# Dense value columns of a retrieval layer: 768 columns in one fp32 product, or 1024 columns in three fp32r products of high and low parts

## The reference

```python
def chunk(zc):                                   # 128 tokens at a time
    ...                                          # expert: (128, 8, 16) indices; gate: softmax of their scores
    u = jnp.take(peer_u, expert, axis=0)
    act = jax.nn.gelu(jnp.einsum('chkd,cd->chk', u, zc))
    v = jnp.take(peer_v, expert, axis=0)
    w = (gate * act.astype(jnp.float32)).astype(zc.dtype)
    return jnp.einsum('chk,chkd->cd', w, v).astype(zc.dtype)
```

## Time and profile before

| | |
|---|---|
| median of 3 runs | 2698.61 us (2697.93 to 2700.31) |
| the profiled execution | 2700.06 us, its span 2698.2 us |
| products, 1535 to 2267 us | DVE busy 667 of 732 us, DMA share 1.01, 419 GB/s |
| dense, 2350 to 2600 us | PE busy 48.7 to 49.6 of each 50 us, DMA share 1.03, 409 GB/s |

### The profile page before, as it was taken

The page is one execution under the profiler, slowest core; times in us unless marked ns, Lnnn a source line. Parts: engine busy times, 40 slices in busy tenths (PEclk is TensorE's granted clock), DMA queues, the critical chain, the costliest instruction groups (busy, mean ns, idle before and its releaser), DMA issues.

```text
span 2698.2 us, 30775 instructions
## 1 busy us (share of the span) xinstructions
PE 2310.5 (86%) x11234; PEld 1779.3 (66%) x11234; DVE 1996.8 (74%) x2973; ACT 850.6 (32%) x1259; POOL 560.1 (21%) x706
## 2 busy tenths in 40 slices
PE   8999989999999999989899965555555656999996
PEld 7997778888888888889788832222233334655553
DVE  6986657665566556587767998889999997766667
ACT  5433555443444344454541111000233332300000
POOL 1000000000000000000002344433443442334375
PEclk9999999999999999999999976666787787999998
DMA  6533445555555655544568999999999997699998
GB/s 224 187 123 104 126 140 183 189 179 191 190 188 179 191 189 172 178 133 151 177 220 361 421 420 419 420 420 420 419 420 416 410 419 295 228 409 409 409 409 343
DMA packets 314373, 747.67 MB, mean 277 GB/s; under 512 B 21028, under 2 KB 223012, under 8 KB 275752
## 3 DMA queue, kind: packets, MB, share of 16 engines
q0 software_dynamic: 73728, 436.24, 39.6%
q1 hardware_dynamic: 240408, 309.21, 34.2%
q10 hardware_dynamic: 144, 1.05, 0.1%
HBM read 744.35 MB, written 2.10 MB: 277 GB/s over the span
## 4 chain that ended last, share of the span: by engine, by line
DMA 24%; DVE 17%; PE 13%; POOL 3%; issue 2%; ACT 1%; DVEq 0%; POOLq 0%
DMA row<-in_peer_u,expert 13%; DMA row<-in_peer_v_rows,expert 11%; DVE row L2430 8%; PE pl L832 4%; PE pl L839 3%; POOL row L770 3%; DVE acc L2441 1%; PE pl L1226 1%; PE pl L835 1%; PE pl L836 1%; DVE hot_b L2467 1%; PE pl L1155 1%; DVE wlo L1883 1%; PE pg L1251 0%; PE pl L1251 0%
## 5 line engine op out<-in xcount | busy, mean ns | idle before, releaser
L1883 DVE TENSOR_TENSOR wlo<-raw,whi 128x1024 fp32r<-128x1024 f32 (+1 forms) x436 | 517.8, 1208 | 374.1 <-ACT whi L1304 372.4
L1226 PE MATMUL pl<-row,diag 128*128 128x512 f32 (+1 forms) x666 | 403.4, 764 | 296.3 <-DMA row<-in_peer_v_rows,expert 283.5
L2430 DVE CUSTOM_DVE_ANT_0 row<-row,pg 128x2048 f32<-128x2048 f32 x256 | 576.7, 2283 | 63.3 <-DMA row<-in_peer_u,expert 62.1
L1304 ACT ACTIVATE whi<-raw 128x1024 fp32r<-128x1024 f32 (+1 forms) x436 | 444.5, 1039 | 411.2 <-PE pl L839 406.6
L1226 PEld LDWEIGHTS pl<-row,diag 128*128 128x128 f32 x666 | 167.4, 268 | 491.3 <-issue 430.3
L832 PE MATMUL pl<-x_split,whi 128*128 128x512 f32 x1888 | 478.6, 395 | 9.5 <-DVE x_split L1891 4.6
L832 PEld LDWEIGHTS pl<-x_split,whi 128*128 128x128 f32 x1888 | 341.6, 190 | 73.8 <-issue 7.5
L839 PE MATMUL pl<-x_split,wlo 128*128 128x256 f32 x2656 | 373.2, 284 | 3.8 <-DVE wlo L1883 3.8
L839 PEld LDWEIGHTS pl<-x_split,wlo 128*128 128x128 f32 x2656 | 358.6, 192 | 23.1 <-DVE wlo L1883 4.4
L770 POOL DMA_INDIRECT row<-in_peer_v_rows,expert x256 | 288.7, 1128 | 340.5 <-DVE acc L2441 147.5
L1259 PE MATMUL pg<-v_tile,spread 128*128 128x512 f32 (+1 forms) x1024 | 335.0, 489 | 4.6 <-DMA v_tile<-in_peer_v_dense 4.6
(11 more groups left out here) (337 smaller groups left out, 2136.5 us busy)
## 6 DMA issues: line engine op xcount, KB each, us to landing
raw<-in_w_in SPq DMA_DIRECT2D x51, 1024.0 KB, 5.2
v_tile<-in_peer_v_dense SPq DMA_DIRECT2D x128, 384.0 KB, 7.3
raw<-in_w_gate SPq DMA_DIRECT2D x44, 1024.0 KB, 5.1
raw<-in_w_up SPq DMA_DIRECT2D x44, 1024.0 KB, 5.1
raw<-in_w_out SPq DMA_DIRECT2D x32, 1024.0 KB, 5.5
raw<-in_w_down SPq DMA_DIRECT2D x32, 1024.0 KB, 5.4
wq<-in_peer_wq SPq DMA_DIRECT2D x15, 1024.0 KB, 11.6
raw<-in_w_down SPq DMA_DIRECT2D x16, 768.0 KB, 4.7
```

Source lines behind the costliest of these rows:

```text
L1226: last = mm(pl_all[:, c:c + width], diag[:, (at - 1) % 4, :], row[b][:, c - DENSE:c - DENSE + width], start=at == 1, stop=at == ADDED_ROWS ...
L1304: return nc.scalar.activation(o, i, ACT.Copy)
L1883: V.tensor_tensor(wlo[:, n % 4, 0:k, :], w[:, :, f, :], whi[:, n % 4, 0:k, :].bitcast(F32), ALU.subtract)\
L2430: V.tensor_tensor_reduce(row[b][:], row[b][:], z_tok[:], 1.0, 0.0, ALU.mult, ALU.add, dots[:, at:at + 1])\
```

## The change

The dense part has 1024 columns instead of 768, and is computed as three fp32r products of high and low parts instead of one fp32 product. In each of the 128 steps ACT rounds the tile (`high_tile`) and two weight blocks (`high_weights`), DVE subtracts to get the tile's low part (`low_tile`, written over the tile), POOL subtracts to get the weights' low part (`low_weights`), and PE runs high x high, high x low, low x high: 12 products of 512 columns. There are 5 tile buffers and 3 for each of the other parts. The gathered rows are 4 KB in place of 5 KB, the late ring has 5 row buffers in place of 6, PE adds 113 rows and DVE sums 143. DVE's sums now stand between its `low_tile` steps, and POOL's gathers between its `low_weights` steps, by `rows_by`. The weights `spread` lie in one tensor `spread_all`, and in the spread stage PE has three PSUM banks in turn.

```diff
-DENSE = 768
+DENSE = 1024
 GATHERED = D - DENSE
 EARLY = 100
-ADDED_ROWS = 111
+ADDED_ROWS = 113
...
+def rows_by(m):
+
+    return min(SUMMED_ROWS, (m + 1) * SUMMED_ROWS // (NKEY - 6))
...
-TILE_HOMES = RING
+TILE_HOMES = RING + 1
+HIGHS = 3
...
             sp.wait_ge(sel_ready, TT * PH)
+            sp.wait_ge(dot_done, PRODUCTS)
+            sp.wait_ge(row_added, EARLY)
             for m in range(NKEY):
                 if m == 1:
 
                     sp.wait_ge(hot_used, TT * GROUPS)
+                    sp.wait_ge(row_added, ADDED_ROWS)
                 elif m >= TILE_HOMES:
                     sp.wait_ge(tile_used, m - TILE_HOMES + 1)
...
+            def low_weights(m):
+
+                pool.wait_ge(spread_high, INPUTS + m + 1)
+                c = slice(m * P, (m + 1) * P)
+                nc.gpsimd.tensor_tensor(spread_lo[m % HIGHS][:], spread_all[:, :, c], spread_hi[:, m % HIGHS].bitcast(F32), ALU.subtract)\
+                    .then_inc(spread_low, 1)
+
+            low = 0
             for j, (table, t, n, k) in enumerate(ROW_ORDER):
+                while j >= ADDED_END and rows_by(low + 1) < j - ADDED_END:
+                    low_weights(low)
+                    low += 1
...
+            for m in range(low, NKEY):
+                low_weights(m)
...
-                for c, width in ((DENSE, 256), (1024, 512), (1536, 512)):
+                for c, width in ((1024, 512), (1536, 512)):
                     last = mm(pl_all[:, c:c + width], diag[:, (at - 1) % 4, :], row[b][:, c - DENSE:c - DENSE + width],
...
             def dense(m):
 
-                pe.wait_ge(tile_full[m % TILE_HOMES], tile_landed(m))
-                for t in range(TT):
-                    for c, width in ((0, 512), (512, DENSE - 512)):
-                        last = mm(pg_all[:, t * 1024 + c:t * 1024 + c + width], spread[t][:, m, :],
-                                  v_tile[m % TILE_HOMES][:, c:c + width], start=(m == 0), stop=(m == NKEY - 1), skip_group_check=True)
-                last.then_inc(tile_used, 1)
+                def part(weights, columns, first, final):
+
+                    for t in range(TT):
+                        for h in range(2):
+                            last = mm(pg[2 * t + h], weights(t), columns[:, h * 512:(h + 1) * 512], start=(first and m == 0),
+                                      stop=(final and m == NKEY - 1), skip_group_check=True)
+                    return last
+
+                high, low = v_hi[m % HIGHS], v_lo[m % TILE_HOMES]
+                w_high = lambda t: spread_hi[:, m % HIGHS, t, :]
+                w_low = lambda t: spread_lo[m % HIGHS][:, t, :]
+                pe.wait_ge(tile_hi, PIECES + m + 1)
+                pe.wait_ge(spread_high, INPUTS + m + 1)
+                part(w_high, high, True, False)
+                pe.wait_ge(tile_lo, PIECES + m + 1)
+                part(w_high, low, False, False)
+                pe.wait_ge(spread_low, INPUTS + m + 1)
+                part(w_low, high, False, True).then_inc(tile_used, 1)
...
+            def high_tile(m):
+
+                if m >= HIGHS:
+                    act.wait_ge(tile_used, m - HIGHS + 1)
+                act.wait_ge(tile_full[m % TILE_HOMES], tile_landed(m))
+                copy(v_hi[m % HIGHS][:], v_tile[m % TILE_HOMES][:]).then_inc(tile_hi, 1)
+
+            def high_weights(m):
+
+                copy(spread_hi[:, m % HIGHS], spread_all[:, :, m * P:(m + 1) * P]).then_inc(spread_high, 1)
+
...
-            for table, t, n, k in ROW_ORDER[ADDED_END:]:
-                sum_row(t, n, k)
-                if (t, n, k) == (1, 0, 7):
-                    add_sums()
+            def low_tile(m):
+
+                dve.wait_ge(tile_hi, PIECES + m + 1)
+                V.tensor_tensor(v_lo[m % TILE_HOMES][:], v_tile[m % TILE_HOMES][:], v_hi[m % HIGHS][:].bitcast(F32), ALU.subtract)\
+                    .then_inc(tile_lo, 1)
+
+            r = 0
+            for m in range(NKEY):
+                low_tile(m)
+                for table, t, n, k in ROW_ORDER[ADDED_END + r:ADDED_END + rows_by(m)]:
+                    sum_row(t, n, k)
+                    if (t, n, k) == (1, 0, 7):
+                        add_sums()
+                r = rows_by(m)
```

More of the change, by code:

```diff
@@ L325, in build @@
         row = [sb(f"row{n}", region, start, [P, D]) for n, (region, start) in enumerate(homes)]
[L326 to L328 removed]
+        homes = [*(("xhi", m * GATHERED) for m in range(4)), ("arena", 3 * D)]
         row += [sb(f"row{len(row) + n}", region, start, [P, GATHERED]) for n, (region, start) in enumerate(homes)]
@@ L337, in build @@
         HOTS = len(hot_homes)
-        spread = [sb(f"spread{t}", region, 0, [P, NKEY, P]) for t, region in enumerate(("raw", "xlo"))]
-        tile_homes = [("spare", 0), ("rest", sq_r_at), ("arena", 4 * D), ("arena", 4 * D + DENSE)]
-        v_tile = [sb(f"v_tile{m}", region, start, [P, DENSE]) for m, (region, start) in enumerate(tile_homes)]
-        gain_homes = [("arena", 4 * D + 2 * DENSE), ("rest", choice_at), ("rest", turned_at), ("rest", sq_sum_at)]
-        gain_row = [sb(f"gain_row{q}", region, start, [P, 512]) for q, (region, start) in enumerate(gain_homes)]
+        spread_all = sb("spread_all", "raw", 0, [P, TT, 5 * 16 * S])
+        spread = [spread_all[:, t, 0:NKEY * P].rearrange("p (i c) -> p i c", i=NKEY) for t in range(TT)]
+        tile_homes = [("arena", 2 * D), ("arena", 4 * D), ("arena", 4 * D + DENSE),
+                      ("rest", choice_at), ("rest", choice_at + DENSE)]
+        high_homes = [("arena", 2 * D + DENSE), ("arena", 3 * D + DENSE), ("rest", choice_at + 2 * DENSE)]
+        v_tile = [sb(f"v_tile{m}", region, start, [P, DENSE]) for m, (region, start) in enumerate(tile_homes)]
+        v_lo = [sb(f"v_lo{m}", region, start, [P, DENSE], F32R) for m, (region, start) in enumerate(tile_homes)]
+        v_hi = [sb(f"v_hi{m}", region, start, [P, DENSE], F32R) for m, (region, start) in enumerate(high_homes)]
+        spread_hi = sb("spread_hi", "spare", 0, [P, HIGHS, TT, P], F32R)
+        low_homes = [("rest", 0), ("rest", TT * P), ("rest", choice_at + 3 * DENSE)]
+        spread_lo = [sb(f"spread_lo{m}", region, start, [P, TT, P], F32R) for m, (region, start) in enumerate(low_homes)]
+        gain_row = sb("gain_row", "raw", 2 * D, [P, D])
         scrap = sb("scrap", "raw", 0, [P, TT, D])
@@ L489, in build @@
         spread_ready = sem("spread_ready")
-        tile_full = slot_full
+        tile_full = [*slot_full, x_in[0]]
+        tile_hi, tile_lo = w_hi, w_lo
+        spread_high, spread_low = x_hi, x_lo
         tile_used = sem("tile_used")
@@ L514, in tile_landed @@
         def tile_landed(m):
-            return 16 * (max(LOADS[u] for u in range(len(LOADS)) if u % RING == m % TILE_HOMES) + m // TILE_HOMES + 1)
+            n = m % TILE_HOMES
+            earlier = max(LOADS[u] for u in range(len(LOADS)) if u % RING == n) if n < RING else 1
+            return 16 * (earlier + m // TILE_HOMES + 1)
         def sq_count(n, t4):
@@ L1244, in spread_group @@
                     pe.wait_ge(first_ready, FIRST_READY + 2 * n + 2)
-                if g > t:
-                    pe.wait_ge(spread_ready, n - t)
+                banks = [pl[0], pl[1], pg[0]] if t else [pl[0], pl[1]]
+                if g >= len(banks):
+                    pe.wait_ge(spread_ready, n - len(banks) + 1)
                 a, b = hot_a[n % HOTS], hot_b[n % HOTS]
-                bank = pg[0] if t and g % 2 else pl[0]
+                bank = banks[g % len(banks)]
                 for c in range(GROUP):
@@ L1777, in spread_copy @@
                 act.wait_ge(hot_used, t * GROUPS + g + 1)
-                bank = pg[0] if t and g % 2 else pl[0]
+                bank = [pl[0], pl[1], pg[0]][g % 3] if t else pl[g % 2]
                 copy(spread[t][:, :, g * GROUP:(g + 1) * GROUP].rearrange("p i c -> p c i"),
@@ L1818, in _ @@
             turned_copy(1)
+            added = ADDED_ROWS - EARLY
             for g in range(GROUPS):
-                if g % 3 == 1 and LATER + g // 3 + 2 < ADDED_END:
-                    weight_matrix(*ROW_ORDER[LATER + g // 3 + 2][1:])
+                at = g * added // GROUPS
+                if (g + 1) * added // GROUPS > at and at + 2 < added:
+                    weight_matrix(*ROW_ORDER[LATER + at + 2][1:])
+                if g == GROUPS - 2:
+                    high_tile(0)
                 spread_copy(1, g)
+            act.wait_ge(spread_ready, TT * GROUPS)
+            high_weights(0)
             activation(small[:, 60:61], halfpi[:], ACT.Sqrt)
@@ L1826, in square @@
                 activation(scrap[:, t, c], acc[:, t, c], ACT.Square, accum_out=small[:, at:at + 1]).then_inc(fin_sq, 1)
-            act.wait_ge(tile_used, TT * D // P)
-            act.wait_ge(sums_ready, 1)
-            square(0, slice(DENSE, D), 41)
+            act.wait_ge(hot_used, TT * GROUPS)
+            act.wait_ge(row_added, ADDED_ROWS)
+            for m in range(1, NKEY):
+                high_tile(m)
```

(4 more changed lines are left out.)

37 lines of the change are left out of this document (17 added, 20 removed).

## The result

The kernel with the change takes 2712.19 us (median of 5 runs, 2711.16 to 2717.25); before takes 2700.31 beside it (5 runs, 2697.93 to 2702.92). The ratio is 1.0049 with an interval of 1.0036 to 1.0062: slower by 0.5%, where 1.6% was forecast. The profiled execution took 2711.48 us, its span 2709.7.

What follows compares the result with a forecast made beforehand. Products stage bound by transfers, dense stage by PE and transfers, then by DVE held off by POOL at 3.30 us a tile. 2700.06 - 27 - 1 + 70.7 = 2742.8, forecast 2742 us; range 2686 to 2805.

Steps and rivals of the forecast that it cites:

- Products stage: Stage bound by transfers: 100 gathered rows at 4 KB instead of 5 KB save 27 us, bounds 18 and 31.
- PE adds 13 rows of 2 products ... I take 1: Spread stage: 13 rows of two 512-column products replace 11 of 512+512+256, about 1 us less.
- PE and transfers: Dense stage, per tile: PE needs 2.76 us for 12 products, transfers 2.785 us for 1.139 MB at 409 GB/s.
- DVE alone: Dense stage: DVE's subtraction and sums, without interference from POOL, take 2.67 us a tile.
- 1.23 + 1.28 - 0.08: Dense stage, DVE: subtraction plus sum less one overlap of neighbours gives 2.43 us a tile.
- the hold: Dense stage: POOL's low_weights reading holds off DVE's two-input instructions, 0.58 us plus 0.05 handing over, making 3.30 a tile.
- The 4 us of the start: Dense stage start: tile 1 must land, be rounded and subtracted after the last added row, 4 us more.
- POOL costs DVE nothing: Rival 1, dense stage: PE and transfers set the pace at 2.85 us a tile, 2688 us, faster; chance 0.18.
- POOL missing its gap: Rival 2, dense stage: POOL waits for a further DVE instruction, 3.75 to 3.8 us a tile, 2803 us; chance 0.2.
- Short rows that save nothing: Rival 3, products stage: DVE at 97% in parts prevents the saving, about 2765 us; chance 0.07 with rival 4.
- a lower clock: Rival 4, dense stage: PE's clock falls, with PE busy 84% in short gaps; chance 0.07 together with rival 3.
- the break-even point: Dense stage: at 2.95 us a tile the whole kernel is no faster than before.

Runs made afterwards that it cites:

- experiment 5: Kernel after with the 100 early gathers at their old 5 KB width, of which PE uses 4 KB: 2743.20 us, ratio 1.0152 to before.
- experiment 6: Kernel before with only one part of the change, three PSUM banks in the second half of the spread stage: 2694.78 us, ratio 0.9976.
- Experiment 1: Kernel after, with POOL writing zeros for the weights' low part instead of subtracting, so it reads nothing there: 2682.21 us.
- experiment 2: Kernel after with DVE's sums accumulated in PSUM, so a sum has one SBUF input: 2688.72 us, ratio 0.9951 to before.
- experiment 8: Kernel after with POOL subtracting only 128 elements and writing zeros to the other half: 2696.22 us, ratio 0.9983 to before.
- experiment 4: Kernel after with POOL's subtraction of the low weights done twice, one after the other: 2866.47 us.
- experiment 7: Sums-in-PSUM kernel with POOL's subtraction held until the tile's own low_tile is done and gathers issued further ahead: 2700.44 us, ratio 0.9999 to before.
- experiment 3: Kernel after with DVE subtracting the low weights right after low_tile, POOL keeping only gathers: 2690.99 us, ratio 0.9965 to before.

## Why the prediction was right in kind and wrong in size

**Products stage, right.** -25.8 us for -27 forecast; experiment 5 gives 26.0 back with the bytes alone, and executions of this stage differ by some us. The worry that DVE's slack might run out was sound but didn't bite: 1.1 of 100 us remain at the tightest place.

**Spread stage, wrong by 5.4 us.** The step "PE adds 13 rows of 2 products ... I take 1" looked at PE's products only. The diff also gave PE a third bank, which I read and didn't cost; experiment 6 measures 4.3 us for it, and 1.1 us of the miss stay without a cause. Before's trace had the hint, small waits of PE for ACT to empty a bank and of DVE for PE.

**Dense stage: PE and transfers, right.** Experiment 1 takes DVE's hold away and what remains is PE at 50 of 50 and transfers at 1.03, period 2.84 for 2.76 and 2.785.

**Dense stage, DVE alone: 2.58 in place of 2.67.** The instructions are 1.215 and 1.275 us long (1.23 and 1.28 forecast), but a tile has two overlaps of neighbours, sum over `low_tile` and `low_tile` over sum, 0.076 and 0.077 in the trace. The step "1.23 + 1.28 - 0.08" counted one. With 0.24 for the second sum in one of six tiles as forecast, 1.215 + 1.275 - 0.153 + 0.24 = 2.58.

**Dense stage, the hold: 0.48 in place of 0.63.** The mechanism is the prediction's, and experiments 1 and 2 show it from both sides. The rate was right too: 2.17 ns an element (experiment 8) for the 2.26 taken from the earlier trace rows. What failed is "0.58 us come on top ..., with some 0.05 for the handing over". No handing over shows, and the sums, 60 of the 96 instructions that are met, lose only 0.44. Per tile of 2345 to 2640 us the means give (1.415 - 1.215) + 1.172 x (1.516 - 1.275) = 0.48, and 2.58 + 0.48 = 3.06, which is the period measured there. Of the 26.8 us by which this stretch came out shorter, 24.4 are the tiles: the 120 from the third `low_tile` on took 3.10 each for 3.30. Another 3.0 are the start, where the sum had 4 us and two tiles of 3.30 to the third `low_tile` and the trace has 7.6 us; the end took 0.6 more. The 4 us of the start were too many, and no run takes them apart.

The timeline shows a part of why a sum loses less than a `low_tile`. The 45 sums that follow a `low_tile` start 0.22 us into the subtraction on average and lose 0.48. The 15 that follow another sum wait for it, start 0.46 us in, when less of the subtraction is left, and lose 0.30. Why the 45 lose 0.06 less than a `low_tile` stays open; POOL's own instruction is 0.89 us there and 0.95 where it meets a `low_tile`.

**The rivals.** That POOL costs DVE nothing (1) is refuted by experiments 1 and 2, though the price came out nearer to it than to the forecast in time: 2688, 2712, 2742. POOL missing its gap (2) isn't what happens here, since PE waits for `v_lo` alone; it is real and near, as experiments 4 and 7 show. Short rows that save nothing (3) are refuted by experiment 5, a lower clock (4) by the 1.00 in the window.

The sign was decided by the break-even point, 2.95 us a tile in the prediction and 2.99 with the 5.4 us that the spread stage gained beyond the forecast (5.4 / 122 = 0.04). After has 3.08. Experiments 2, 3 and 8, with 2.88, 2.94 and 2.95, lie below it and beat before; experiment 7, with 3.00, equals it.

**What stays open.** The 7 us of experiment 5's dense stage, the last 0.06 us of the sums' smaller loss, the 3 us at the start of the dense stage, and what decides whether a `low_tile` that is already running is held. Experiment 2 together with 3, which would remove POOL's reading and keep the PSUM accumulator, wasn't run.

## What to carry to other kernels

Before elementwise work goes to POOL because it has room, charge its reading time (2.17 ns an element here) to DVE if DVE's instructions there have two SBUF inputs: at 256 elements that was 0.48 us, against 0.34 for doing the work on DVE. Where it must run on POOL, let one of DVE's operands live in PSUM (11 us below before instead of 12 above). And when a stage is bound by an engine that runs without a break, count its overlaps at both ends of each instruction, and cost every hunk of the diff: 0.1 us a tile and one PSUM bank were a half of the error's size here, 12 and 4 us of 31.

## What the runs showed of the hardware that I had not expected

The hold is lopsided. In the kernel after a POOL subtraction makes DVE's next two-input instruction longer, a POOL gather never does (0 of 96), while the gather itself is held: 1.76 us for 93 of 113 in the kernel after, for 0.94 where no two-input DVE instruction is running when it starts. In experiment 2 the 52 gathers (2345 to 2640 us) that started in a sum with its accumulator in PSUM took 0.95 us each.

And a little more POOL work is not a little more time: one more subtraction a tile, 0.75 us undisturbed, raised the period by 1.34, from 3.08 to 4.42 (experiment 4). There POOL's instructions are all longer than undisturbed, while PE waits for POOL's result and DVE for the rows that POOL issues.
